# A two-layer float32 block on one core: activations stationary with 512 weight columns to a matmul, and one low part in four of the feed-forward's up stages on VectorE

## What is computed

```python
def rmsnorm(x, g):
    y = xf * lax.rsqrt(jnp.mean(xf * xf, axis=-1, keepdims=True) + EPS)
    return (y * g.astype(jnp.float32)).astype(x.dtype)

def swiglu(u, w_gate_up, w_down):          # width 1024 -> 2 x 2816 -> 1024
    gate, up = jnp.split(u @ w_gate_up, 2, axis=-1)
    return (jax.nn.silu(gate) * up) @ w_down
...
h = h + FFN_RES_WEIGHT * swiglu(rmsnorm(h, ffn1_norm[i]), ffn1_w_gate_up[i], ffn1_w_down[i])
```

## Time and profile before

| | |
|---|---|
| time, median of 3 runs | 1801.54 us (1800.02 to 1802.3) |
| span of the profiled execution, first to last instruction | 1799.0 us |
| PE matmul busy | 1637.3 us, 91% |
| PE weight loads busy | 1582.9 us, 88% |
| POOL busy | 1181.1 us, 66% |
| ACT busy | 786.7 us, 44% |
| DVE busy | 704.7 us, 39% |
| mean granted clock of TensorE | 0.950 |

### The profile page before, as it was taken

The page is one execution under the profiler, slowest core; times in us unless marked ns, Lnnn a source line. Parts: engine busy times, 40 slices in busy tenths (PEclk is TensorE's granted clock), DMA queues, the critical chain, the costliest instruction groups (busy, mean ns, idle before and its releaser), DMA issues.

```text
span 1799.0 us, 31209 instructions
## 1 busy us (share of the span) xinstructions
PE 1637.3 (91%) x12670; PEld 1582.9 (88%) x12670; DVE 704.7 (39%) x952; ACT 786.7 (44%) x1009; POOL 1181.1 (66%) x496
## 2 busy tenths in 40 slices
PE   6999899999979788989999896876999989989998
PEld 5999899999968688989999886866999986689997
DVE  2221154246179422332222497564223366522211
ACT  4444443465443333444444493123444343344442
POOL 5888687888745366478867665303888854168884
PEclk9999999999989889999999997998999998899999
DMA  5555444554534233435544444002454533035551
GB/s 222 178 177 207 163 162 167 185 177 177 189 140 141 75 140 137 141 136 176 180 155 171 146 146 152 1 1 81 164 181 176 182 117 117 5 138 187 187 180 54
DMA packets 37745, 261.27 MB, mean 145 GB/s; under 512 B 4204, under 2 KB 5016, under 8 KB 6808
## 3 DMA queue, kind: packets, MB, share of 16 engines
q1 hardware_dynamic: 34704, 249.58, 39.2%
q10 hardware_dynamic: 2952, 10.39, 1.6%
HBM read 258.86 MB, written 1.09 MB: 145 GB/s over the span
## 4 chain that ended last, share of the span: by engine, by line
PE 59%; POOL 17%; DVE 11%; issue 10%; ACT 3%; DMA 0%; POOLq 0%; ACTq 0%; DVEq 0%
POOL t L379 17%; PE bank L429 16%; PE bank L430 16%; PE bank L431 16%; PE bank L509 2%; DVE t L1177 1%; PE bank L549 1%; PE bank L706 1%; PE bank L718 1%; PE bank L572 1%; PE bank L717 1%; DVE t L1164 1%; DVE t L1595 1%; DVE t L1433 0%; DVE t L1291 0%
## 5 line engine op out<-in xcount | busy, mean ns | idle before, releaser
L379 POOL TENSOR_TENSOR t<-t,t 128x1024 fp32r<-128x1024 f32 x474 | 1155.1, 2442 | 558.5 <-ACT t L820 558.1
L429 PE MATMUL bank<-t,t 128*128 128x256 f32 (+1 forms) x3664 | 1057.5, 289 | 90.5 <-DVE t L1186 55.4
L430 PE MATMUL bank<-t,t 128*128 128x256 f32 (+1 forms) x3664 | 1051.4, 287 | 0.0
L431 PE MATMUL bank<-t,t 128*128 128x256 f32 (+1 forms) x3664 | 1050.4, 287 | 0.0
L820 ACT ACTIVATE t<-t 128x1024 fp32r<-128x1024 f32 x474 | 498.4, 1058 | 731.1 <-PE bank L431 695.7
L429 PEld LDWEIGHTS bank<-t,t 128*128 128x128 f32 x3664 | 718.6, 196 | 99.1 <-issue 83.3
L430 PEld LDWEIGHTS bank<-t,t 128*128 128x128 f32 x3664 | 719.1, 196 | 0.3
L431 PEld LDWEIGHTS bank<-t,t 128*128 128x128 f32 x3664 | 718.4, 196 | 0.0
L1199 DVE TENSOR_TENSOR t<-t,bank 128x512 f32<-128x512 f32 x44 | 30.3, 689 | 354.1 <-PE bank L431 354.1
L1205 DVE TENSOR_TENSOR t<-t,t 128x512 f32 (+1 forms) x44 | 101.5, 2307 | 39.9 <-ACT t L894 39.9
L1218 DVE SCALAR_TENSOR_TENSOR t<-bank,t 128x512 f32<-128x512 f32 x16 | 11.0, 692 | 208.8 <-PE bank L431 208.5
(11 more groups left out here) (206 smaller groups left out, 1225.3 us busy)
## 6 DMA issues: line engine op xcount, KB each, us to landing
t<-in_w SPq DMA_DIRECT2D x237, 1024.0 KB, 4.8
t<-acs_scratch ACTq DMA_DIRECT2D x8, 512.0 KB, 3.7
t<-in_mem ACTq DMA_DIRECT2D x2, 1024.0 KB, 4.8
t<-gdn_scratch ACTq DMA_DIRECT2D x1, 1536.0 KB, 6.3
t<-in_x ACTq DMA_DIRECT2D x1, 1024.0 KB, 7.7
out<-t SPq DMA_DIRECT2D x4, 256.0 KB, 2.4
t<-in_lvl ACTq DMA_DIRECT2D x1, 448.0 KB, 3.1
t<-in_band ACTq DMA_DIRECT2D x1, 256.0 KB, 3.3
```

The costliest lines, as they stand in the source:

```text
L379: nc.gpsimd.tensor_tensor(half(w_lo[k % SPLIT], hf), half(raw[k % RAW], hf), half(w_hi[k % SPLIT], hf).bitcast(F32), ALU.subtract).then_in ...
L429: mm(o, lhi, rhi, start=start, stop=False, **kw)
L430: mm(o, lhi, rlo, start=False, stop=False, **kw)
L431: return mm(o, llo, rhi, start=False, stop=stop, **kw)
```

## The change

The activations become the stationary operand (128 tokens, called s = 0 and s = 1, by 128 features) and the weights the moving one. The stream is cut into 474 pieces of 128 x 1024; ten raw slots (`w_lo` is written over the raw slot) and six `w_hi` slots replace the former buffers. `ORDER` gives each stage a kind:

- `pair` (up stages, gate_a, short_out, gate_b, mem_v, mem2v), `proj` (mix, xo, wo0, wo1) and `acc` (the four down stages and ssm_out): matmuls of 512 columns. Two neighbouring chunks are taken together, 256 columns of each; a chunk takes 24 matmuls. These are 132 + 42 = 174 chunks.
- `row` (62 chunks) and `nat` (1): still 256 columns, 48 matmuls a chunk.

Results of the first group lie as tokens x features. The residual x is now kept so too. Thus the product of gate and up must be turned before the down stage: `hid_turn` (4 PE transposes for each pair of chunks), then ACT `hid_hi` and DVE `hid_lo` read the turned bank. The norms sum along the free dimension on ACT (`square` with an accumulator); for `ffn0` to `ffn3` the factor 1/rms is applied behind the matmuls (scale of Silu, scalar of the product). Each norm is made for s = 0 and then for s = 1, with 8 transposes each (`turn`) and 8 small ACT and 8 small DVE instructions. In the up stages DVE makes the low part of each fourth piece (`ON_DVE`), POOL the other three. The loops on the engines are written out in full. The parts of the diff are, in this order, the numbers, POOL's low parts, PE's helpers and its up stage, ACT's `feed` and its up stage (`after(q)` is `feed(q + 1 + HI)`, so it rounds up to the piece q + 6), and DVE's up stage.

```diff
+RAW, HI = 10, 6
+ON_DVE = {P0[f"ffn{_f}_up"] + 4 * _j + 3 for _f in range(4) for _j in range(11)}
...
-                pool.wait_ge(hi_made, c2 + (hf + 1))
-                nc.gpsimd.tensor_tensor(half(w_lo[k % SPLIT], hf), half(raw[k % RAW], hf),
-                                        half(w_hi[k % SPLIT], hf).bitcast(F32), ALU.subtract).then_inc(split_done, 1)
+                for q in range(a, n):
+                    if q in ON_DVE:
+                        continue
+                    pool.wait_ge(hi_made, q + 1)
+                    nc.gpsimd.tensor_tensor(w_lo[:, q % RAW, :], raw[:, q % RAW, :],
+                                            w_hi[:, q % HI, :].bitcast(F32), ALU.subtract).then_inc(split_done, 1)
...
+            def split_through(q):
+                pe.wait_ge(split_done, POOL_N[q])
+                if DVE_N[q] and (q - 1 in ON_DVE or q - 2 in ON_DVE):
+                    pe.wait_ge(split_dve, DVE_N[q])
...
+            def half_pair(b, hi, lo, s, q, ready=None):
+                h = PIECES[q][1]
+                for k in range(4):
+                    kt = 4 * h + k
+                    if ready:
+                        ready(s, kt)
+                    c = slice(k * S, k * S + S)
+                    a = slice(s * P, s * P + P)
+                    mm(b[:], hi[:, kt, a], w_hi[:, q % HI:q % HI + 2, c], start=kt == 0, stop=False)
+                    mm(b[:], hi[:, kt, a], w_lo[:, q % RAW:q % RAW + 2, c], start=False, stop=False)
+                    m = mm(b[:], lo[:, kt, a], w_hi[:, q % HI:q % HI + 2, c], start=False, stop=kt == KT - 1)
+                return m
...
+            def hid_turn(f, j):
+                pe.wait_ge(row_free, G0[f"ffn{f}_up"] + 2 * j + 2)
+                if 11 * f + j:
+                    pe.wait_ge(W["ffn_lo"], 11 * f + j)
+                for t in range(2):
+                    for s in range(2):
+                        m = nc.tensor.transpose(bank[TB][:, t, s * P:s * P + P], hid[j % 2][:, s, t * P:t * P + P], ident[:])
+                m.then_inc(W["ffn_t"], 1)
...
             def ffn(f, between, ready, before_down=None, halfway=None):
+                for j in range(11):
+                    for h in range(2):
+                        q = P0[name] + 4 * j + 2 * h
+                        split_through(q + 2)
+                        for s in range(2):
+                            r = 2 * j + s
+                            if h == 0 and r >= 3:
+                                pe.wait_ge(row_free, G0[name] + r - 2)
+                            m = half_pair(bank[FB[r % 3]], u_hi, u_lo, s, q, ready if j == 0 else None)
+                            if s:
+                                m.then_inc(piece_done, 2)
+                            elif h:
+                                m.then_inc(s0_done, 1)
+                            if j == 0 and h == 0:
+                                between(s)
+                            elif h == 0 and s:
+                                hid_turn(f, j - 1)
...
             def feed(n):
+                for q in range(fed[0], min(n, NPIECE)):
+                    act.wait_ge(raw_landed[q % RAW], 16 * (q // RAW) + 16)
+                    if q >= HI:
+                        act.wait_ge(piece_done, q - HI + 1)
+                    fn(w_hi[:, q % HI, :], raw[:, q % RAW, :], ACT.Copy).then_inc(hi_made, 1)
...
             def ffn(f, early, before_down=None):
+                for j in range(11):
+                    a = P0[name] + 4 * j
+                    after(a - 1)
+                    if j == 0:
+                        early()
+                        act.wait_ge(n_rs, 2 * STAT[norm] + 2)
+                    after(a)
+                    if j:
+                        hid_hi(f, j - 1)
+                    after(a + 1)
+                    gate(j, 0)
+                    gate(j, 1)
...
             def ffn(f, before_down=None):
+                for j in range(11):
+                    if j:
+                        hid_lo(f, j - 1)
+                    for s in range(2):
+                        if s == 0:
+                            q = P0[name] + 4 * j + 3
+                            dve.wait_ge(hi_made, q + 1)
+                            v.tensor_tensor(w_lo[:, q % RAW, :], raw[:, q % RAW, :], w_hi[:, q % HI, :].bitcast(F32), ALU.subtract).then_inc(split_dve, 1)
+                        dve.wait_ge(W["ffn_act"], 22 * f + 2 * j + s + 1)
+                        v.scalar_tensor_tensor(out=hid[j % 2][:, s, :], in0=bank[FB[(2 * j + s) % 3]][:, 1, :],
+                                               scalar=stat_of(norm, "rstd")[:, s:s + 1], in1=act_g[j % 2][:, s, :],
+                                               op0=ALU.mult, op1=ALU.mult).then_inc(row_free, 1)
```

More of the change, by code:

```diff
@@ L103, in build, with place @@
         names = [0]
-        def place(shape, dt, kb):
+        def place(name, shape, dt, kb):
             names[0] += 1
[L108 to L115, removed]
@@ L143, in build @@
[L143 to L153, removed]
@@ L163, in build @@
[L163 to L171, removed]
-        kb = place([P, 6, S], F32, HB + 12)
-        gbc = place([P, 12, S], F32, HB)
@@ new lines, in x_at, with stat_of, turn_banks @@
+        def x_at(name, s):
+            change = NORM[name][0]
+            k = UPDATES.index(change)
+            return 4 * k + (4 if s else 3 if KIND.get(change) == "proj" else 2)
+        def stat_of(name, what):
+            o = 6 * (STAT[name] % 2) + 2 * ("sum", "root", "rstd").index(what)
+            return stats[:, o:o + 2]
+        def turn_banks(name):
+            if name in ("ffn1", "ffn2", "ffn3", "mix_a", "out"):
+                return [4, 5, 6, 7]
+            g = G0[{"mix": "gate_a", "xattn": "xq", "kv": "kv_v"}[name]]
+            return [(g + 2) % 4, (g + 3) % 4, 4, 5]
@@ new lines, in turn @@
+            def turn(name, s, src=x):
+                i = TURN[name]
+                if src is x:
+                    pe.wait_ge(x_up, x_at(name, s))
+                for k4 in range(2):
+                    if src is not x:
+                        pe.wait_ge(n_xn, 4 * XN[name] + 2 * s + k4 + 1)
+                    for kt in range(4 * k4, 4 * k4 + 4):
+                        m = nc.tensor.transpose(turned(name, s, kt), src[:, s, kt * P:kt * P + P], ident[:])
+                    m.then_inc(n_t, 1)
@@ L1053, in _ @@
-            act.wait_ge(unit_done, U0["l2"])
+            after(P0["ssm_out"] + 13)
+            for s in range(2):
+                for d in range(2):
+                    i = 2 * s + d
+                    act.wait_ge(W["mg_t"], i + 1)
+                    fn(four(u_hi, d, s), quads(bank[(G0["xq"] + i) % 4]), ACT.Copy).then_inc(W["m_hi"], 1)
+                after(P0["ssm_out"] + 14 + s)
+            after(P0["mix"] + 3)
+            square("xattn", 0)
+            root("xattn", 0)
+            normalised("xattn", 0)
@@ new lines, in _ @@
+            square("xattn", 1)
+            root("xattn", 1)
+            normalised("xattn", 1)
+            after(P0["xq"] - 3)
+            hi_part("xattn", 0, "xattn_norm")
+            hi_part("xattn", 1, "xattn_norm")
+            after(P0["xo"] - 1)
+            run(attention("xatt", 1.0 / 16, pr_x))
+            after(P0["xo"] + 3)
+            square("ffn1", 0)
+            hi_part("ffn1", 0, "ffn2_norm")
+            after(P0["xo"] + 5)
+            act.wait_ge(unit_done, U0["gfin"])
@@ L1251, in taps @@
                                 cnt += 1
-                    after(j)
+                    then(j)
                 return cnt
```

1275 lines of the change are left out of this document (733 added, 542 removed), and 4 rows, old and new, of the table PLAN.

## The result

The change makes the kernel slower: 1991.67 us (median of 4 runs, 1991.21 to 1992.32) against 1801.57 us, a ratio of 1.106 (95% interval 1.104 to 1.107). The profiled execution's span is 1989.4 us, 190.4 above the one before.

A forecast was written before the change was run, and what follows sets the result against it. PE was taken to set the pace in the stages, POOL 0.4 us behind, with PE standing at norms between them. Terms -100 + 20 + 188 + 80 - 15 = +173 us on the 1799.0 span gave 1972, forecast median 1975 us, range 1880 to 2050.

The forecast's parts named there:

- The new wait: Up stages: PE stalls 4.7 us for DVE's low part in 40 passes, +188 us (148 to 236).
- The clock: Behind each of the 40 stalls PE runs at half clock, losing 2.0 us each, +80 us (68 to 100).
- Wider matmuls: Matmuls of 512 columns at 0.216 us save 0.58 us in each of 174 chunks, -100 us.
- My bound of no saving: Bound on wider matmuls: nothing saved if the load's extra 0.013 us adds to the columns at each half.
- Turning the product: Four PE transposes, 44 times at 0.46 us each, +20 us.
- the rival by which wide matmuls are faster than their columns: POOL's 2.44 us then holds each piece, 153 us saved in place of 100: 1922 us; chance 0.03.
- Norms and start: 5 us saved at each of three norms ahead of up stages, other norms and start even: -15 us (-40 to +20).
- The mixers' norms: Among the five other norms, which lose their sums but get two chains in a row on ACT: taken as even.
- the one without the wait: Rival: DVE's piece is ready in time and PE does not stall, 1706 us; chance 0.02.
- POOL as the bound: Rival: outside the up stages POOL loses 0.1 to 0.2 us in some 260 pieces, +40, 2015 us; chance 0.05.
- the stall at full clock: Rival: the up-stage stalls come but the half clock does not, 1895 us; chance 0.15.
- the norms' win: Rival: all ten waits at norms vanish, 126 us saved, stall at its lower bound, full clock: 1744 us; chance 0.07.

The follow-up runs named there:

- experiment 4: The change with 17 more matmuls of 512 columns behind each turn of the product, into a bank nobody reads: 1913.37 us, ratio 1.063.
- experiment 1: The change with POOL making all four low parts of a pass in the up stages and DVE none: 1724.25 us, ratio 0.957.
- experiment 2: The change with DVE's weight piece ahead of the turned product's low part, same work on each engine: 1733.03 us, ratio 0.962.
- experiment 3: The change with ACT's high part of the turned product ahead of its weight piece, DVE's order kept: 1864.98 us, ratio 1.035.
- experiment 6: The change with the product's turn 2.7 us earlier and ACT's high part of it ahead of its weight piece: 1800.66 us, ratio 1.000.
- experiment 5: The kernel of experiment 1 with each matmul of 512 columns as two of 256: 1772.37 us, ratio 0.985.
- experiment 11: The kernel of experiment 1 with each turn of the product made twice into the same bank: 1737.10 us, ratio 0.966.
- experiment 7: The kernel of experiment 1 with x of s = 1 turned ahead of the up stages of ffn1, ffn2 and ffn3: 1723.09 us, ratio 0.958.
- experiment 8: The kernel of experiment 2 with POOL making the fourth piece's low part in each up stage's first pass: 1723.77 us, ratio 0.958.
- experiment 10: The change with 12 more matmuls behind each turn of the product, into a bank nobody reads: 1911.99 us, ratio 1.063.
- experiment 9: The change with 8 more matmuls behind each turn of the product, into a bank nobody reads: 1958.74 us, ratio 1.088.

## Why the prediction was right where it was

The forecast was 1975 us and the time is 1992. Its mechanism is shown. Two of its terms were mis-sized in opposite directions, one by 50 us and one by 27, so that the sum came within 17 us is partly luck.

- **The new wait, +188: right.** At full clock the stall costs 16.02 - 11.37 = 4.65 us a pass (experiments 4 and 1), 186 us for 40 passes. Experiment 2 shows that the order makes it, experiment 3 that ACT's place in the chain counts, experiments 3 and 6 that DVE's and POOL's instructions with SBUF operands wait for each other.
- **The clock, +80: right.** Experiment 4 gives 78 us. Behind 30 of the 40 waits the clock was low for about 3.4 us, which cost 1.3 to 1.6 us, and behind ten for twice as long, which cost 2.8. That split was not foreseen, and 2.0 is near its mean.
- **Wider matmuls, -100: the step that failed.** I took 0.216 us a matmul from the passes over ones, with the load hidden under the columns. My bound of no saving had the 0.013 us over the columns added once to each 256 columns. The truth lies between: it is added once to each matmul, wide or narrow, so a wide one takes 0.227 us, and half the saving is lost. By the direct price (experiment 5) the term is -50. What the 0.013 us are, and why the passes over ones did with 0.217, stays open. The Trainium skill ("TensorE: Matmul & The Clock Gate", "Back-to-back issue gap") has 216 ns for an isolated gap and 131 ns for a sustained stream at 512 columns. The measured 0.227 us is above both, and the rival by which wide matmuls are faster than their columns is out.
- **Turning the product, +20: right**, 18.5 by experiment 11.
- **Norms and start, -15: too small.** What is left of the 190.4 us is 190.4 + 50 - 18.5 - 186 - 78 = -42. The earlier trace rows stand at the norm ahead of `xq` and not, as their heading and the prediction say, at the one ahead of `ffn1`. That one took the same 10.1 us in the kernel before:

```profile
761.08 0.28 PE L431 MATMUL bank<-t,t 128*128 128x256 f32 x1
...
771.16 0.55 PE L429 MATMUL bank<-t,t 128*128 128x256 f32 x1 [6.34 <-DVE t L1186]
```

  From the start of the last addition to x ahead of `ffn1` (761.40 before, 735.54 in experiment 1) to that of the last one behind it (971.95 and 930.81), experiment 1 takes 195.3 us in place of 210.5. Wide matmuls and turns account for 33 x 0.29 - 11 x 0.42 = 5 of the 15, so the norm gave 10 us and not 5. The rows say why: the projection's last matmul starts at 735.06, the first of the up stage at 735.29, and PE stands only 1.70 us ahead of 740.75, with the clock at 1.00 behind it, where the prediction had 5 us for the waits and 1.7 for the clock:

```profile
735.06 0.39 PE L461 MATMUL bank<-w_hi,h_lo 128*128 128x512 f32 x1
735.29 0.39 PE L459 MATMUL bank<-w_hi,u_hi 128*128 128x512 f32 x1
...
738.01 1.03 PE L537 MATMUL bank<-ident,x 128*128 128x128 f32 x8
740.75 0.50 PE L459 MATMUL bank<-w_hi,u_hi 128*128 128x512 f32 x1 [1.70 <-DVE u_lo L1390]
```

  Experiment 7 shows that this is not due to the second turn's place. That it is due to the first half's chain, which runs under the projection's last part, is only read from the rows and not shown. In the change itself the first DVE piece takes some of this back: PE waits for it 2.24 us in `ffn1` (until 812.97), and experiment 8 prices it at 9 us in all stages together.

  The same reckoning over the other stretches of experiment 1 gives 9 us for the norm of `ffn2` and 8 for that of `ffn3`, so 27 for the three and not 15. The mixers' norms, which were taken as even, were not: less their wide matmuls, the stretch from `ffn0` to the norm ahead of `xq` is 16 us shorter, that from `ffn1` to `ffn2` 15 us shorter, and that from `ffn2` to `ffn3` 9 us longer, at a mean clock of 0.81 in place of 0.87. What shortened the two was not tried.

Of the other rivals, the one without the wait is ruled out by the forty waits, POOL as the bound by experiment 1, the stall at full clock by the granted clock of 0.66 and experiment 4, and the norms' win by the result. The best versions are experiments 1, 7 and 8 (1723 to 1724 us), which can't be told apart, 4.2 to 4.3% faster than before.

## What to carry to other kernels

Before an engine is given a piece of another's work, read its rows ahead of that piece back to the engine that will wait for it: if one of them waits for something that this engine issues just ahead of its own wait, the chain is closed. It then costs its whole length each time, and half clock on top where PE stands long enough. Here 44 instructions, 1.2 us each when nothing holds them, cost 267 us in one order and 9 in the other (experiments 1 and 2), and weren't needed. A wider matmul saves only the part of a matmul's time that isn't columns, here 0.013 us for each matmul fewer, so price it by the distance of starts of a real stream.

## What the hardware showed

- PE idle and its granted clock: behind 1.6 to 1.7 us idle (experiments 6 and 10) it never fell in 80 waits, behind 4.4 us (the change) in all 40, and behind 2.6 us in 15 of 40 (experiment 3) or 30 of 40 (experiment 9). Behind 2.2 us it fell too, in the kernel before (PE resumed at 563.56) and in the change (at 812.97). A fall lasts about 3.4 us and costs 1.3 to 1.6, or twice as long and costs 2.8. It doesn't begin at the same place each time: in the pass shown it came about 0.9 us after PE had gone on.
- A DVE and a POOL instruction that both have both inputs in SBUF: the one that starts later ends about its own time alone behind the other's end (1.08 and 1.09 us for DVE's piece, 2.23 for POOL's), as if it had waited for the whole of it. DVE's piece took 1.22, 2.38 or 2.93 us by when it started, POOL's 2.4 or 3.07. With one input in PSUM, DVE's low part took its 0.69 us while POOL's instruction ran (103.48 in the change).
- In a stretch of small matmuls the granted clock can stay at 0.50 for 20 us. With the same work that stretch took 142.2 us in one kernel and 136.3 in another that reached it 15 us later (experiments 1 and 11), and 134.1 in the kernel before at a mean clock of 0.87. What decides it was not tried.
